# A two-block transformer kernel: how the triangular factors of the first mixer are inverted

## The reference

```python
decay = jnp.exp(jnp.where(causal, g[..., :, None] - g[..., None, :], -jnp.inf))
lmat = jnp.where(strict, jnp.einsum('bhncd,bhnsd->bhncs', k_beta, k) * decay, 0.0)
t_inv = lax.linalg.triangular_solve(eye + lmat, jnp.broadcast_to(eye, lmat.shape),
                                    left_side=True, lower=True, unit_diagonal=True)
u = jnp.einsum('bhncs,bhnsd->bhncd', t_inv, v_beta)
```

## Time and profile before

| | |
|---|---|
| time, median of 3 runs | 1308.55 us (1308.27 to 1310.14) |
| span of the profiled execution | 1308.4 us |
| time of the nearest run to that span | 1308.27 us |
| TensorE products, weight loads | 1266.0 us (97%), 909.2 us (69%) |
| VectorE, ScalarE, GpSimd | 567.2 us (43%), 239.2 us (18%), 111.8 us (9%) |
| mean granted clock of TensorE | 0.993 of full speed |

### The profile page before, as it was taken

One profiled execution on the slowest core, in us unless ns is written; L12 is line 12 of the kernel. 1 busy time (PEld: TensorE's weight loads), 2 busy tenths in 40 slices (PEclk: granted clock), 3 DMA queues, 4 the chain that ended last, 5 costly groups with the idle time before them and its releaser, 6 DMA issues.

```text
span 1308.4 us, 25634 instructions
## 1 busy us (share of the span) xinstructions
PE 1266.0 (97%) x11215; PEld 909.2 (69%) x11215; DVE 567.2 (43%) x1070; ACT 239.2 (18%) x502; POOL 111.8 (9%) x109
## 2 busy tenths in 40 slices
PE   7999999999999999899999999999989979999997
PEld 6888986899984458447566666666647646998443
DVE  0653644456789866324201110111061254555545
ACT  1461342123120012502001010100021031111000
POOL 1036102500001000000200000000133000000000
PEclk9999999999999999898999999999999999999999
DMA  9963220557565581837999999999997240353520
GB/s 344 350 217 97 65 98 1 120 158 187 150 222 192 151 123 26 314 123 289 381 417 412 407 407 415 415 407 407 403 346 221 84 173 1 129 194 142 193 116 32
DMA packets 119820, 292.09 MB, mean 223 GB/s; under 512 B 6268, under 2 KB 66144, under 8 KB 107456
## 3 DMA queue, kind: packets, MB, share of 16 engines
q1 hardware_dynamic: 107584, 270.29, 57.6%
q0 software_dynamic: 4800, 14.67, 3.7%
q10 hardware_dynamic: 7360, 6.03, 1.5%
HBM read 274.19 MB, written 16.78 MB: 222 GB/s over the span
## 4 chain that ended last, share of the span: by engine, by line
PE 91%; DVE 4%; ACT 2%; DMA 1%; issue 1%; SPq 0%; POOL 0%; DVEq 0%; ACTq 0%; POOLq 0%
PE bank L2571 18%; PE bank L2349 9%; PE bank L2021 9%; PE bank L2588 9%; PE bank L2743 8%; PE bank L2781 7%; PE bank L2034 6%; PE bank L2356 6%; PE bank L2506 4%; PE bank L1993 3%; PE bank L2432 2%; PE bank L2165 1%; PE bank L2455 1%; PE bank L2151 1%; PE bank L2205 1%
## 5 line engine op out<-in xcount | busy, mean ns | idle before, releaser
L2571 PE MATMUL bank<-arena 128*32 128x352 f32 x3072 | 231.1, 459 | 1.4 <-DVE arena L1359 0.7
L2571 PEld LDWEIGHTS bank<-arena 128*32 128x32 f32 x3072 | 144.2, 110 | 85.2 <-issue 6.0
L2021 PE MATMUL bank<-xT,arena 128*128 128x256 f32 x608 | 135.8, 383 | 2.2 <-ACT arena L1690 1.4
L2021 PEld LDWEIGHTS bank<-xT,arena 128*128 128x128 f32 x608 | 115.8, 192 | 18.5 <-ACT arena L1690 1.8
L2588 PE MATMUL bank<-arena 128*32 128x256 f32 x2112 | 117.1, 379 | 0.0
L1404 DVE TENSOR_TENSOR arena<-arena,bank 128x352 f32<-128x352 f32 x24 | 19.2, 798 | 204.3 <-PE bank L2571 179.1
L2588 PEld LDWEIGHTS bank<-arena 128*32 128x32 f32 x2112 | 78.1, 110 | 36.6
L2781 PE MATMUL bank<-arena 128*128 128x512 f32 x224 | 96.7, 592 | 0.7 <-DVE arena L1532 0.7
L2349 PE MATMUL bank<-xT,arena 128*128 128x128 f32 x704 | 83.2, 275 | 0.5 <-DVE arena L1189 0.5
L2349 PEld LDWEIGHTS bank<-xT,arena 128*128 128x128 f32 x704 | 80.8, 192 | 2.0 <-issue 1.3
L2781 PEld LDWEIGHTS bank<-arena 128*128 128x128 f32 x224 | 42.3, 190 | 53.6 <-issue 49.5
(11 more groups left out here) (424 smaller groups left out, 1476.1 us busy)
## 6 DMA issues: line engine op xcount, KB each, us to landing
arena<-moe_w SPq DMA_DIRECT2D x64, 1408.0 KB, 16.5
arena<-moe_w SPq DMA_DIRECT2D x24, 1536.0 KB, 18.4
arena<-ffn_w SPq DMA_DIRECT2D x44, 512.0 KB, 6.6
arena<-gdn_w_in SPq DMA_DIRECT2D x8, 2048.0 KB, 20.2
arena<-w_up SPq DMA_DIRECT2D x8, 2048.0 KB, 8.7
arena<-w_down SPq DMA_DIRECT2D x8, 2048.0 KB, 7.5
arena<-ffn_w SPq DMA_DIRECT2D x11, 1024.0 KB, 5.0
slot_rows<-arena SPq DMA_DIRECT2D x1, 9600.0 KB, 48.7
```

What stands on the lines that cost most here:

```text
L2021: last = mm(bank[:, at:at + SEQ], w[:, k, P * m:P * m + P], x[:, k, :], start=(k == 0), stop=(k == KT - 1))
L2571: last = mm(banks[i][32 * q:32 * q + 32, 0:EW1], xg[:, t, EK * s + kk], w[:, kk, EW1 * q:EW1 * q + EW1], start=(s == 0 and kk == 0), stop= ...
```

## The change

The levels 0 to 3 (block sizes 1, 2, 4, 8) leave TensorE. The 16 factors have 8 diagonal blocks of 16 x 16 each, 128 blocks in all, and there are 128 partitions. `key_products` no longer writes D: four copies, one for each 32 partitions, collect the diagonal 32 x 32 blocks of four factors in `low_c`. `small_inverses`, all on VectorE, turns them in 32 x 32 blocks (`V_.transpose`) so that each partition holds one whole 16 x 16 block, inverts it there by doubling from size 2 to 16 with elementwise products and sums over the innermost axis, and brings it back in two more transposes: `DT_c` (the inverse, transposed) and `D_c`, compact diagonal 32 x 32 blocks.

TensorE does level 16 with 32 x 32 pieces on the four diagonal quadrants (64 products for Q, 64 for P), level 32 with 32 x 32 pieces in two quadrants (32 and 32 products), level 64 with 64 x 64 pieces (16 and 16). No factor is turned on TensorE: VectorE transposes, and ScalarE spreads the compact blocks into DT and D64, which GpSimd has zeroed. Input products 25 and 26 stand between the levels, the key transposes come before the last P, the value transposes after it. The value convolution of GpSimd waits no longer for the key products. The constants table has 7 matrices instead of 14.

```diff
-        D, DT, QT = region(16384, 16, P), region(18432, 16, P), region(38984, 16, P)
+        DT = region(18432, 16, P)
+        low_c, turned_c = region(16384, 16, 16, 2), region(16896, 16, 32)
+        rows_of, cols_of = region(17408, 16, 2, 16), region(17920, 16, 2, 16)
+        D_c, DT_c, Q_c = (region(38984 + 512 * i, 16, 32) for i in range(3))
...
+            pool.wait_ge(conv_done, 4)
+            nc.gpsimd.memset(DT, 0.0).then_inc(inv_zeroed, 1)
+            pool.wait_ge(ss_ready, NT)
+            nc.gpsimd.memset(D64, 0.0).then_inc(inv_zeroed, 1)
             pool.wait_ge(vec_ok, 1)
-            pool.wait_ge(kq_read, 4)
...
+                V_.tensor_tensor(decT[:, s], four(banks[2 + j % 2]), decT[:, s], ALU.mult).then_inc(kq_read, 1)
+                dve.wait_ge(kq_read, j + 1)
+                for q in range(4):
+                    last = V_.tensor_copy(low_c[quadrant(q), :, s].rearrange("p c b i -> p b i c"), decL[quadrant(q), s, quadrant(q)].rearrange("p b (i c) -> p b i c", i=2))
+                return last
+
+            def small_inverses():
+
+                even, odd, minus_even, minus_odd = (mat(C_EYE)[:, 16 + i:17 + i] for i in range(4))
+                link(V_.transpose(turned_c, low_c.rearrange("p c b i -> p c (b i)")))
+                turned_low = neg_low.rearrange("p r c -> p c r")
+                link(V_.tensor_scalar(turned_low, turned_c[:, :, 0:16], minus_even, None, ALU.mult))
+                link(V_.scalar_tensor_tensor(turned_low, turned_c[:, :, 16:32], minus_odd, turned_low, ALU.mult, ALU.add))
+                link(V_.tensor_copy(cells(inv16, 1, (34, 8)), cells(neg_low, 16, (34, 8))))
+                for n in (2, 4, 8):
+                    k = 8 // n
+                    each_sum = terms16[:, 0:k * n * n * n].rearrange("p (a s) -> p a s", s=n)
+                    for i in range(k):
+                        last = V_.tensor_tensor(cells(terms16, n * n * n * i, (n * n, n), (n, n), (1, n)), cells(neg_low, 34 * n * i + 16 * n, (0, n), (16, n), (1, n)),
+                                                cells(inv16, 34 * n * i, (16, n), (0, n), (1, n)), ALU.mult)
+                    link(last)
+                    link(V_.tensor_reduce(partial16[:, 0:k * n * n], each_sum, AX, ALU.add))
+                    for i in range(k):
+                        last = V_.tensor_tensor(cells(terms16, n * n * n * i, (n * n, n), (n, n), (1, n)), cells(inv16, 34 * n * i + 17 * n, (0, n), (1, n), (16, n)),
+                                                cells(partial16, n * n * i, (n, n), (0, n), (1, n)), ALU.mult)
+                    link(last)
+                    link(V_.tensor_reduce(cells(inv16, n, (34 * n, k), (16, n), (1, n)), each_sum, AX, ALU.add))
+                for i, sel in enumerate((even, odd)):
+                    last = V_.tensor_scalar(rows_of[:, :, i], inv16.rearrange("p c r -> p r c"), sel, None, ALU.mult)
                 link(last)
+                V_.transpose(DT_c.rearrange("p b (i r) -> p r b i", i=2), rows_of.rearrange("p r i c -> p r (i c)").rearrange("p r (b i) -> p r b i", i=2)).then_inc(inv16_ready, 1)
+                for i, sel in enumerate((even, odd)):
+                    last = V_.tensor_scalar(cols_of[:, :, i], inv16, sel, None, ALU.mult)
+                link(last)
+                V_.transpose(D_c.rearrange("p b (i c) -> p c b i", i=2), cols_of.rearrange("p c i r -> p c (i r)").rearrange("p c (b i) -> p c b i", i=2)).then_inc(inv16_ready, 1)
...
+            for hf in range(2):
+                s = slice(8 * hf, 8 * hf + 8)
+                dve.wait_ge(lv_p, hf + 1)
+                V_.tensor_tensor(DT_c[:, s], DT_c[:, s], compact(banks[2 + hf])[:, 0:8], ALU.subtract).then_inc(lv_pe, 1)
+            dve.wait_ge(lv_pe, 2)
+            V_.transpose(D_c.rearrange("p a b -> p (a b)"), DT_c.rearrange("p a b -> p (a b)")).then_inc(inv16_ready, 1)
...
+            link(V_.tensor_scalar(corner_c[32:64].rearrange("p a b -> p (a b)"), banks[1][0:32, :], -1.0, None, ALU.mult))
+            V_.transpose(D64[32:64, :, 0:32], corner_c[32:64]).then_inc(inv16_ready, 1)
...
-            dve.wait_ge(vk_tr, 4)
+            dve.wait_ge(vk_tr, 6)
...
+            take_silu(4)
+            take_z(24)
+            act.wait_ge(inv_zeroed, 2)
+            act.wait_ge(lv_pe, 2)
+            spread(2)
+            spread(3).then_inc(d_spread, 1)
+            act.wait_ge(inv16_ready, 3)
...
+            take_z(25)
+            take_silu(5)
+            take_z(26)
...
+            z_product(24)
+
+            for hf in range(2):
+                pe.wait_ge(inv16_ready, 1)
+                for b in range(8 * hf, 8 * hf + 8):
+                    for q in range(4):
+                        d = quadrant(q)
+                        last = mm(compact(banks[hf])[d, b % 8], decL[d, b, d], DT_c[d, b], start=True, stop=True)
+                last.then_inc(lv_q, 1)
+            pe.wait_ge(inv16_ready, 2)
+            for hf in range(2):
+                pe.wait_ge(lv_qe, hf + 1)
...
+            z_product(25)
+            pe.wait_ge(lv_pe, 2)
+            for i in range(2):
+                up, low = corner(i)
+                for b in range(16):
+                    last = mm(compact(banks[4 + i])[up, b], decL[low, b, up], DT_c[low, b], start=True, stop=True)
+                last.then_inc(lv_q, 1)
+            z_product(26)
...
+            pe.wait_ge(inv16_ready, 4)
+            for j in range(2):
+                key_turn(j)
+            pe.wait_ge(d_spread, 2)
...
+                if j >= 2:
+                    pe.wait_ge(lv_pe, 3 + j)
+                value_turn(j)
```

More of the change, by code:

```diff
@@ L56 @@
 MASKED = -1e30
[L59 to L63, removed]
+C_ID, C_TRI, C_LOW, C_ONE, C_REV, C_EYE, C_IOTA = range(7)
 N_CONST = C_IOTA + 1
@@ L496, in s5_pool, with cells, quadrant, corner @@
                 last.then_inc(im_ready, 1)
[L498 to L512, removed]
+        def cells(ap, offset, *steps):
+            return bass.AP(ap.tensor, ap.offset + offset, [list(ap.ap[0]), *[list(x) for x in steps]])
+        def quadrant(q):
+            return slice(32 * q, 32 * q + 32)
+        UPPER, LOWER = ((64, 96), (0, 32)), ((96, 128), (32, 64))
+        def corner(i):
+            return slice(*UPPER[i]), slice(*LOWER[i])
+        def compact(bank):
+            return bank[:, :].rearrange("p (a b) -> p a b", b=32)
+        def halves64(bank):
+            return bank[0:64, :].rearrange("p (a b) -> p a b", b=64)
         @block.sync
@@ L878, in _ @@
             key_products(1)
+            V_.memset(terms16, 0.0)
+            link(V_.memset(inv16, 0.0))
+            V_.memset(cells(inv16, 0, (17, 16)), 1.0)
             key_products(2)
[L880 to L898, removed]
@@ L2188, in _ @@
-            pe.wait_ge(lv_pe, 24)
+            z_product(24)
+            for hf in range(2):
+                pe.wait_ge(inv16_ready, 1)
[5 more added lines that the diff above has]
+            pe.wait_ge(inv16_ready, 2)
+            for hf in range(2):
+                pe.wait_ge(lv_qe, hf + 1)
+                for b in range(8 * hf, 8 * hf + 8):
+                    for q in range(4):
+                        d = quadrant(q)
+                        last = mm(compact(banks[2 + hf])[d, b % 8], D_c[d, b], Q_c[d, b], start=True, stop=True)
+                last.then_inc(lv_p, 1)
@@ new lines, in key_turn, with value_turn @@
+            def key_turn(j):
+                for h in range(4 * j, 4 * j + 4):
+                    last = transpose(four(banks[j])[:, h % 4], qkvT[:, 8 + h, 0:P])
+                last.then_inc(vk_tr, 1)
+            def value_turn(j):
+                for b in range(4 * j, 4 * j + 4):
+                    last = transpose(four(banks[(4, 5, 2, 3)[j]])[:, b % 4], qkvT[:, 16 + b % 8, P * (b // 8):P * (b // 8) + P])
+                last.then_inc(vk_tr, 1)
+            low64 = slice(64, 128)
+            pe.wait_ge(lv_pe, 3)
```

148 lines of the change are left out of this document (63 added, 85 removed).

## The result

| | before | after |
|---|---|---|
| time, median | 1308.55 us (1308.27 to 1310.14) | 1293.74 us (1288.16 to 1297.34) |
| ratio, 95% interval | | 0.987 [0.985, 0.989] |
| span of the profiled execution | 1308.4 us | 1290.7 us |
| TensorE products, weight loads | 1266.0, 909.2 us | 1235.2, 831.7 us |
| VectorE, ScalarE, GpSimd | 567.2, 239.2, 111.8 us | 570.4, 231.2, 115.2 us |

The kernel is 14.8 us faster by the medians and 17.7 us by the spans. Forecast were 34.1 us, and the time lies above the range. Each run's time is its span plus 1.8 us (1290.7 belongs to a run of 1292.5), so the span of before, 1308.4, belongs to the run of 1310.14; the table ahead of the prediction had put a wrong run beside it.

The account below looks back on a forecast made before the run. TensorE, holding 91% of the span, was taken as the bound. Product 27 moving from 178.05 to about 143.9 us took 34.1 us off 1308.4, giving 1274.3, stated as 1274.5 us; range 1269.5 to 1283.

Parts of the forecast that it names:

- Off the path: Work beside the stage on GpSimd, ScalarE and transfers, including the earlier value convolution, done at 130 us: costed at nothing.
- Product 27: First input product after the inversion stage: starts at about 143.9 us instead of 178.05, 34.1 us less.
- Product 24 ends near 119.4: Input product ahead of level 16: ends at 119.4 us, after 2.8 and 6.9 us leave the front.
- TensorE idles under 1 us before level 16: Wait between product 24 and level 16: first factor ready at 120.05 us, 0.7 after product 24.
- rival (b): VectorE's small inverses take 16 us instead of 11, TensorE idles 5 to 9 us more: 1279.5 to 1284; chance 0.16.
- the chain: VectorE's linked small-inverse steps, from 109.05 us to the first factor: 11.0 us, bounds 8.3 to 16.
- 256 instructions take 4.4 us: Level 16 on TensorE, 2 x 64 products at 17 ns a start: 4.35 us, bounds 3.3 to 8.7.
- Idle of 0.4 us ahead of the key transposes: TensorE waits near 0.4 us before the key transposes, a wait ended by VectorE.
- Silu 5 or GpSimd ahead of the value transposes: Sign of a wrong forecast: either one releases TensorE before the value transposes; no size given.
- Rival (c): Granted clock falls around the small pieces from 134 to 142 us: 1277 to 1281 us; chance 0.09.
- Rival (e): Levels 32 and 64: pieces in the same array rows don't overlap, 58 us instead of 8.6: 1324 us; chance 0.02.
- (f): Spread, silu or a hidden wait binds TensorE for about the saved time: near 1308 us; chance 0.01.

Follow-up runs that it names:

- both remedies together: Changed kernel with low_c copies on ScalarE, GpSimd's convolution steps 3 to 6 after the inverses, weight loads after level 16, product 25 between its Q and P: 1275.97 us.
- the version with the loads later: Changed kernel with low_c copies on ScalarE, GpSimd's convolution steps 3 to 6 after the inverses, feed-forward weight loads moved behind level 16: 1281.99 us.

## Why the prediction was wrong

**The failed step is "Off the path".** It put the convolution's earlier start at nothing and named only the harm that VectorE could do to GpSimd, with 10 us of room. Its times were right (start forecast at 99.5 and 116.8, end at 130; measured 97.6, 115.0 and 129.0, and with the 1.8 us of the next paragraph 99.4, 116.8 and 130.8). The direction of the harm was wrong: GpSimd went on nearly undisturbed (1.90 and 2.35 us beside the slow copies, as in the earlier trace rows), and VectorE waited. The Trainium skill describes this ("SBUF — State Buffer", section "🔬 SBUF: two separate sides", under "Who interferes with whom"): one pair of ports is shared by VectorE and GpSimd as an exclusive lock, taken for the whole of an instruction; VectorE needs it for two on-chip inputs beside a GpSimd instruction that reads the on-chip memory, and for its fast copies and tensor_scalar, while tensor_reduce on this chip never contends. The rows agree: copies, products with two inputs and masked copies were held, while L883 keeps its 0.69 us beside GpSimd and steps that read a bank keep theirs. That VectorE was held is measured; that the lock is the reason is the page's account, which these rows fit. The trace of before could not show the collision at this place, because the removed wait prevented it; that was the reason to ask what the wait had kept apart.

**The account.** The stage starts 1.8 us earlier in this execution (`square_sums` at 87.56 instead of 89.38), so 1.8 us are added to each time of after. (Over all eleven executions it starts between 87.6 and 91.1.) Product 27 was forecast at 143.9; it came at 155.78 + 1.8 = 157.6, 13.7 us late. Of these, level 16 started at 130.36 + 1.8 = 132.2 instead of 120.1: 12.1 us, the contention. From there to product 27 it took 25.4 instead of 23.8 us: 1.6. The spans differ from the forecast by 1290.7 - 1274.3 = 16.4 us: 13.7, less the 1.8, plus 4.5 behind product 27, where this execution took 1290.7 - 155.78 = 1134.9 us and before 1308.4 - 178.05 = 1130.4. The changed kernel's second execution took 1130.9 there, and both remedies together 1130.8. So the 4.5 us are no fixed cost of the change. Whether the change makes such executions likelier (its four runs spread over 9 us, those of before over 2) and why the clock was lower there is open.

**Point by point.** "Product 24 ends near 119.4": 117.55 + 1.8 = 119.4, right, and with it what was removed in front. "TensorE idles under 1 us before level 16": 12.81, wrong, though the sign named for rival (b), a transpose as releaser, was there. It was not (b)'s mechanism: undisturbed, the chain takes 10.0 us against 11.0 forecast, and the copies 1.12 against 1.7. Rival (b) saw an end (1279.5 to 1284) that lies below the measured time as well, so the missing case was a rival for contention, with a price. "256 instructions take 4.4 us": 128 take 1.31 at full clock and 1.93 at half clock, so 2.6 us in all, cheaper than the 17 ns a start; level 32 2.11 for each half (2.2) and level 64 2.07 (2.1), right. "Idle of 0.4 us ahead of the key transposes": 0.21, ended by VectorE, right. "Silu 5 or GpSimd ahead of the value transposes": not in the changed kernel, but 3.03 us where the convolution was held back entirely. Rival (c), the clock, came true in kind: product 25 lost 0.9 us in the changed kernel and 1.1 to 2.5 in other versions, behind gaps. Rival (e), products in the same rows of the array, is refuted by levels 32 and 64 (64 in 2.11 us and 32 in 2.07, so 33 and 65 ns each where it needed 222), and (f) did not occur.

**What the sum lacked besides** is the gap of 2.0 us inside P. It was in no row of before, and the prediction has no term for the time in which TensorE's instructions come in. It ate, together with the clock, what the small pieces gave (4.35 - 2.6 = 1.7 us) and 1.6 us more.

**What the mechanism was worth.** With the convolution, the copies, the loads and product 25 each in another place, the kernel is at 1275.97 us, 35.1 us under the kernel before measured beside it. In the stage itself, from `square_sums` to product 27, it takes 52.1 us where before took 88.7 and the changed kernel 68.2: 36.6 us less. The 34.1 us of the forecast were there to be had, but not in the order that the change put the work in.

## What to carry to other kernels

When a change removes a wait or moves a long GpSimd instruction, list the VectorE instructions that will then run beside it, and charge each that has two on-chip inputs, or copies from on-chip memory to on-chip memory, with up to one GpSimd instruction; sums and steps that read a bank are free of it. A wait that looks superfluous may keep two engines apart, so ask what it separated before it is costed at nothing. Look at the queue of kind "instruction" where TensorE stands still without a releaser. Break bursts of very small products with larger ones, and keep bulk transfers away from them; here only both together closed the gaps.

## What the runs showed of the hardware

- A VectorE copy of 0.28 us beside GpSimd instructions of 1.9 and 2.36 us took 1.7 to 2.4 us, one for each of them; four took 8.09 instead of 1.12. GpSimd lost little in the changed kernel (at worst 2.67 instead of 2.36 us for L713 and 2.44 instead of 1.90 for L712).
- TensorE stood still for 1.4 to 3.8 us at the same place of its instruction stream in eight executions, 164 instructions behind product 24, whether these were small pieces alone, idle products before them or a full product among them; in one case again 128 products further on. Every one of the nine gaps ended 1.37 to 1.54 us behind the end of a 16 KB packet of the queue "instruction". The packet came later beside bulk transfers (3.17 against 1.56 us, and 4.05 against 1.25, behind the first piece of level 16). Why 1.4 us pass from its end to the next product is open.
- The granted clock fell towards the level of 1.2 GHz (0.57 and 0.64 as means of two stretches) behind such a gap even when TensorE had been kept busy until 0.8 us before the small pieces, and it stayed at 1.00 in the version without gaps. It also fell without a gap: to 0.50 from 139 to 148 in the version with the loads later, with TensorE busy for 9.00 of 9.00 us. What lowers it there is open. Small pieces took 10 ns each at full clock and 15 ns at half (1.31 and 1.93 us for 128).
- Strided f32 patterns on VectorE were cheaper than doubled: a copy of 128 elements that writes with a stride of 32 took 0.28 us, as a contiguous one (which read a bank), a transpose of 512 with strided writes 1.05 against 0.71, a product of 512 with one strided input 1.02 against 0.69.
